# Neighbourhood attention in a two-layer diffusion step: steps of one query block for both heads of a pair, score products in turn on the two halves of the array's rows

## The chip, the cores and the metric

The kernel runs on one core of one Trainium2 chip, as one program launched once. The metric is the device time of that core in microseconds (us): the median over runs, smaller is better. TensorE is PE in the profile (its weight loads PEld), VectorE is DVE, ScalarE is ACT, GpSimd is POOL, SyncE is SP.

## What is computed

Two layers of a hybrid backbone over 640 tokens of width 1024: 512 latent tokens (an 8 by 64 grid) and 128 context tokens. Each layer is a norm and a modulation, one wide input projection, two mixers side by side (retention and neighbourhood attention), gates, an output projection and a SwiGLU feed-forward. The change lies in neighbourhood attention alone. Cut to what matters, for 8 heads of 64 features:

```python
# latent tokens: a window of 8 rows x 16 columns, and 128 cached context keys
s_loc = einsum('bwhd,bwkhd->bhwk', q, k_window) + bias
s_ctx = einsum('bwhd,bshd->bhws', q, k_ctx)
p = softmax(concatenate([s_loc, s_ctx], -1))
o = einsum('bhwk,bwkhd->bwhd', p[..., :n], v_window) + einsum('bhwk,bkhd->bwhd', p[..., n:], v_ctx)
# the 128 context tokens attend to one another
p = softmax(einsum('bqhd,bkhd->bhqk', q, k)); o = einsum('bhqk,bkhd->bqhd', p, v)
```

All inputs are float32. Each large product is made of three reduced-precision ones: both operands are split into a high and a low part (`...h`, `...l`), and high*high, high*low and low*high are added up.

## The kernel before

**Engines and order.** It is written by hand in one function, `build`, with one instruction stream for each engine and semaphores between them. The order on each engine is the order of the code.

**Weights.** They come in 276 slabs of 128 x 1024 (512 KB), 138 a layer, in the order in which PE uses them. SP starts the transfer of slab i into `raw[slot[i]]` (L826) as soon as the slab that last used this slot is done (`prior[i]`, L360 to L368). ACT makes the high part (`wh`, L942), DVE the low part (`wl`, L1280), both by calls of `split(n)` that stand at fixed places of their streams. `wl` and `raw` of a slot are the same memory. Four slots (0 to 3) are always there; four more (4 to 7) lie over memory that neighbourhood attention uses, and are open from slab `WIDE` = 58 of a layer on. Slabs 40 and 41 of a layer are the queries and keys of the first pair of heads, 42 to 45 the values of all heads (two slabs for each call of `values()`), 46 to 53 eight further columns of 128 outputs that are computed inside the attention loop, 54 and 55 two gate columns behind it, 56 and 57 the first half of the attention's output projection.

**Ahead of the loop.** PE runs two columns and then `values()` twice, each some 14 us. ACT and DVE turn the first values into high and low parts, then make a `split(2)` (ACT L942), which is slabs 46 and 47, then split the cached values and keys (L1141, L1143), ACT negates the biases (`negative_bias`, L1115) and loads the table of Exp (L1147), and only then do both take the second values (`nv`, L1129). PE's first score waits for the release of the second values' unit.

**The loop.** For each layer it takes 40 steps g (4 pairs, 2 heads, 5 blocks): four blocks of 128 latent queries and one block of the 128 context queries. A step on PE is `score(g)` (L630: into bank `sc[g % 2]`), some pieces of a column, `turn(g - 1)` (L650: transposes of the probabilities into `tp[g % 2]`), and on some steps `weigh(head, group)` (L661: probabilities by values). A head has 64 features, so its score products use 64 of the array's 128 rows. A block has 3 or 4 tiles of 128 keys, the last of them the cached context; the context block has one. The column pieces (`half_columns`, L613) are 32 a pair: 8 for each half of two columns, each of three products of 128*128 by 320. They are the queries and keys of the next pair, and for the last pair two gate columns. `pieces` (L347) tells how many are due in a step, `LIN_AT` when ACT and DVE take a finished half from one of two banks (`lin_free`).

DVE adds the bias and takes the minimum in one instruction (L1598), ACT does the exponential with its sum (L1167), DVE takes the reciprocal and multiplies (L1602, L1604), PE transposes, ACT makes the high part (`pth`, L1191), DVE the low part (`ptl`, L1290). ACT and DVE add the two halves of each head's output (L1180, L1613). `split` calls in the loop: 2 at g = 0, then 1 at g = 8, 13, 18, 23, 28, 33 and 38.

POOL loads each head's biases whole (640 KB) into one of two buffers.

Of the kernel before, what the change touches and what calls it, by code (L numbers as in the profile page):

```python
# [7 lines left out]
P = 128  # L8
# [7 lines left out]
NPAIR = 4  # L16
# [13 lines left out]
WIDE, W_O, LAST = 58, 64, 130  # L30
# [28 lines left out]
STEPS = NPAIR * 10  # L59
# [47 lines left out]
def build(nc, x_in, w_main, w_first, w_ada, params, decay, state_in, ctx_k, ctx_v, biases, ccol, cvec,  # L107
# [3 lines left out]
    with ctx:  # L111
# [118 lines left out]
        bias = [n0(f"bias{i}", [P, BIASW]) for i in range(2)]  # L230
        s_at = n0.p - Z
# [5 lines left out]

        n1 = Map(ada_at)
        pth = n1("pth", [P, 2, 2, NS], F32R); ptl = n1("ptl", [P, 2, 2, NS], F32R)
# [71 lines left out]
        bias_in = [sem(f"bias_in{i}") for i in range(2)]  # L311
# [29 lines left out]
        STREAMS = ((0, slice(0, NS)), (1, slice(NS, T)))  # L341
        EARLY, CONSTS = 16 * 4, 16 * 3
# [4 lines left out]
        def pieces(p, v):  # L347

            return min(32, -(-(v + 1) * 33 // 10)) if p < NPAIR - 1 else min(32, -(-(v + 1) * 8 // 3))


        LIN_AT = [[3, 5, 7, 10]] * (NPAIR - 1) + [[3, 6, 9, 12]]

        def halves_at(g):

            return [(p, h) for p in range(NPAIR) for h in range(4) if p * 10 + LIN_AT[p][h] == g]

# [27 lines left out]
        def _(pe):  # L385
# [127 lines left out]
            for l in range(DEPTH):  # L513
# [116 lines left out]
                def score(g):  # L630
                    p, v = divmod(g, 10)
                    hh, j = divmod(v, 5)
                    if g >= 2:
                        pe.wait_ge(s_ready, l * STEPS + g - 1)
                    if p >= 1 and v < 2:
                        pe.wait_ge(lin_free[v], l * 8 + 2 * p)
                    nqh, nql, nkh, nkl = nqk[p % 2]
                    rows = slice(64 * hh, 64 * hh + 64)
                    if j < 4:
                        first, tiles, _ = BLOCKS[j]  # L640
                        n = tiles * P
                        q = [t[rows, j * P:(j + 1) * P] for t in (nqh, nql)]
                        product(sc[g % 2][:, 0:n], q, [t[rows, first * P:first * P + n] for t in (nkh, nkl)], True, True)
                        mm = product(sc[g % 2][:, n:n + P], q, [t[rows, p, :] for t in (ckh, ckl)], True, True)
                    else:
                        mm = product(sc[g % 2][:, 0:P], [t[rows, NS:T] for t in (nqh, nql)],
                                     [t[rows, NS:T] for t in (nkh, nkl)], True, True)
                    mm.then_inc(nsc_ready, 1)

                def turn(g):  # L650
                    j = g % 5
                    pe.wait_ge(d_ready, l * STEPS + g + 1)
                    if g >= 2:
                        pe.wait_ge(pt_ready, l * STEPS + g - 1)
                    tiles = [BLOCKS[j][0] + i for i in range(BLOCKS[j][1])] + ["ctx"] if j < 4 else [4]
                    for i, t in enumerate(tiles):
                        to = PLACE[j][t] if j < 4 else 0
                        mm = pe.transpose(tp[g % 2][:, to * P:(to + 1) * P], s[:, g % 2, i * P:(i + 1) * P], ident[:, :])
                    mm.then_inc(t_ready, 1)

                def weigh(head, group):  # L661


                    pe.wait_ge(pt_ready, l * STEPS + head * 5 + (2, 4, 5)[group])
                    if group == 0:
                        pe.wait_ge(av_free, l * 2 * NPAIR + head)

                    def vals(t):
                        return (cv_ if t == "ctx" else nv[:, t])[:, head // 2, head % 2 * 2:head % 2 * 2 + 2, :].rearrange("p b n -> p (b n)")

                    if group == 2:
                        parts = [(vals(4), av[:, 1, 0:P], pch[:, :], pcl[:, :])]
                    else:
                        odd = (1, 0)[group]
                        only = av[:, 0, (group * 2 + odd) * P:(group * 2 + odd + 1) * P]
                        both = av[:, 0, group * 2 * P:(group * 2 + 2) * P]
                        parts = [(vals("ctx"), both, pth[:, group, :, 0:P], ptl[:, group, :, 0:P]),
                                 (vals(2 - group), only, pth[:, group, odd, 3 * P:], ptl[:, group, odd, 3 * P:])]
                        for i in range(2):
                            at_ = slice((i + 1) * P, (i + 2) * P)  # L680
                            parts.append((vals(group * 2 + i), both, pth[:, group, :, at_], ptl[:, group, :, at_]))
                    for i, (val, out, hi, lo) in enumerate(parts):
                        pe.matmul(out, val, hi, start=i == 0, stop=False)
                        mm = pe.matmul(out, val, lo, start=False, stop=i == len(parts) - 1)
# [1152 lines left out]
```

## Time and profile before

| what | before |
|---|---|
| median of 3 runs | 2387.56 us (2384.54 to 4027.47) |
| the profiled execution: its own time | 2394.6 us |
| its span, first to last instruction | 2392.8 us |
| PE busy | 2295.8 us, 96% of the span |
| PE weight loads busy | 2138.3 us, 89% |
| DVE busy | 1303.6 us, 54% |
| ACT busy | 856.7 us, 36% |
| POOL busy | 85.8 us, 4% |
| mean granted TensorE clock | 0.985 |

Neighbourhood attention (first score to first column behind the loop) stands at 476.95 to 614.10 us in the first layer and at 1642.36 to 1777.84 us in the second. To read it: PE is busy nearly always, so the time is what PE is given to do plus the stretches in which it waits. Matmul records overlap, since matmuls are pipelined: the distance between the starts of two neighbours says what one costs, its own duration does not.

### The profile page before, as it was taken

To read this page: it belongs to the slowest core of one execution; us is meant where nothing else is said; L and a number is where in the kernel's file an instruction comes from. 1 tells how busy PE (TensorE), PEld (TensorE's weight loads), DVE (VectorE), ACT (ScalarE), POOL (GpSimd) and SP (SyncE) were. 2 spreads that over 40 slices of the span, in tenths; PEclk is the share of its full clock that TensorE was granted. 3 is DMA by queue.
4 is the path that set the end of the run, shared out by engine and by line. 5 is a ranking of instruction groups with operands and counts; after the bars stand their busy time and mean duration, and the time that the engine had idled before them with its cause. 6 is when DMAs were issued, how large, how long until landed. Compare 5 with 4: busy or idle time off the path is not lost.

```text
span 2392.8 us, 33465 instructions
## 1 busy us (share of the span) xinstructions
PE 2295.8 (96%) x14296; PEld 2138.3 (89%) x14296; DVE 1303.6 (54%) x1867; ACT 856.7 (36%) x1359; POOL 85.8 (4%) x161
## 2 busy tenths in 40 slices
PE   7999988999989999999979999999999999999997
PEld 3999988988978999999969999999989799999996
DVE  3555567566756767667464555424655534343344
ACT  4544432245335212221265444324553432221212
POOL 0000001000000000000000000000000000000000
PEclk9999999999999999999999999999999999999999
DMA  5211145322443443433412111222222322222121
GB/s 240 84 62 58 58 143 180 104 82 66 164 106 123 156 144 125 158 123 124 106 45 80 58 62 58 71 91 80 82 89 90 116 80 80 73 69 83 59 88 44
DMA packets 59747, 233.57 MB, mean 98 GB/s; under 512 B 7312, under 2 KB 7344, under 8 KB 57424
## 3 DMA queue, kind: packets, MB, share of 16 engines
q1 hardware_dynamic: 41040, 153.12, 19.7%
q0 software_dynamic: 18560, 78.33, 9.5%
q8 instruction: 113, 1.85, 0.3%
q14 instruction: 34, 0.28, 0.0%
HBM read 223.00 MB, written 8.42 MB: 97 GB/s over the span
## 4 chain that ended last, share of the span: by engine, by line
PE 80%; DVE 10%; ACT 4%; issue 2%; DMA 2%; DVEq 1%; ACTq 0%; SPq 0%; POOL 0%; POOLq 0%
PE unit L402 15%; PE unit L403 15%; PE unit L405 15%; PE unit L390 9%; PE unit L392 9%; PE unit L391 9%; DVE junk L1380 2%; DMA raw<-w_main 1%; PE unit L483 1%; DVE rs L1414 1%; PE sc L390 1%; PE unit L519 1%; DVE wl L1280 1%; DVE ptl L1290 1%; PE sc L392 1%
## 5 line engine op out<-in xcount | busy, mean ns | idle before, releaser
L402 PE MATMUL unit<-hmh,wh 128*128 128x320 f32 x2304 | 696.5, 310 | 11.6 <-DVE vl L1290 10.4
L403 PE MATMUL unit<-hml,wh 128*128 128x320 f32 x2304 | 694.0, 309 | 0.0
L1280 DVE TENSOR_TENSOR wl<-raw,wh 128x1024 fp32r<-128x1024 f32 x276 | 335.2, 1222 | 411.3 <-ACT wh L942 405.1
L405 PE MATMUL unit<-hmh,wl 128*128 128x320 f32 x2304 | 525.0, 309 | 0.0
L402 PEld LDWEIGHTS unit<-hmh,wh 128*128 128x128 f32 x2304 | 432.6, 188 | 16.4 <-issue 14.4
L403 PEld LDWEIGHTS unit<-hml,wh 128*128 128x128 f32 x2304 | 432.7, 188 | 2.0
L405 PEld LDWEIGHTS unit<-hmh,wl 128*128 128x128 f32 x2304 | 385.4, 188 | 0.0
L942 ACT ACTIVATE wh<-raw 128x1024 fp32r<-128x1024 f32 x276 | 283.8, 1049 | 118.8 <-DMA raw<-w_main 118.6
L1380 DVE CUSTOM_DVE_ANT_0 junk<-ada,csb,par 128x1024 f32<-128x1024 f32 x160 | 205.5, 1284 | 24.9 <-DMA ada<-w_ada 4.4
L390 PE MATMUL unit<-wh,hmh 128*128 128x256 f32 (+1 forms) x640 | 203.0, 317 | 10.9 <-DVE hml L1290 4.7
L392 PE MATMUL unit<-wh,hml 128*128 128x256 f32 (+1 forms) x640 | 200.8, 314 | 0.0
L391 PE MATMUL unit<-wl,hmh 128*128 128x256 f32 (+1 forms) x640 | 200.7, 314 | 0.0
L390 PE MATMUL unit<-wh,hidh 128*128 128x512 f32 x440 | 172.9, 393 | 0.0
L392 PE MATMUL unit<-wh,hidl 128*128 128x512 f32 x440 | 172.6, 392 | 0.0
L391 PE MATMUL unit<-wl,hidh 128*128 128x512 f32 x440 | 172.5, 392 | 0.0
L1237 ACT ACTIVATE sig<-unit 128x640 f32<-128x640 f32 (+2 forms) x46 | 31.1, 681 | 384.2 <-PE unit L405 380.2
L390 PE MATMUL unit<-hmh,wh 128*128 128x320 f32 (+2 forms) x384 | 131.6, 343 | 14.4 <-DVE hml L1290 14.4
L390 PEld LDWEIGHTS unit<-wh,hmh 128*128 128x128 f32 x640 | 123.6, 193 | 20.1 <-DVE wl L1280 5.1
L1242 ACT ACTIVATE hidh<-sig 128x640 fp32r<-128x640 f32 x44 | 32.5, 739 | 287.5 <-DVE sig L1680 287.5
L392 PEld LDWEIGHTS unit<-wh,hml 128*128 128x128 f32 x640 | 123.5, 193 | 7.3
L391 PEld LDWEIGHTS unit<-wl,hmh 128*128 128x128 f32 x640 | 123.3, 193 | 7.2
L1697 DVE TENSOR_TENSOR mix<-unit,mix 128x1024 f32<-128x1024 f32 x80 | 97.8, 1223 | 46.0 <-PE unit L392 46.0
(283 smaller groups left out, 3461.2 us busy)
## 6 DMA issues: line engine op xcount, KB each, us to landing
raw<-w_main SPq DMA_DIRECT2D x276, 512.0 KB, 3.6
ada<-w_ada POOLq DMA_DIRECT2D x80, 512.0 KB, 3.9
bias<-biases POOLq DMA_DIRECT2D x16, 640.0 KB, 5.1
first<-w_first SPq DMA_DIRECT2D x8, 1024.0 KB, 21.1
x<-x POOLq DMA_DIRECT2D x2, 2560.0 KB, 11.9
gains<-g_rows POOLq DMA_DIRECT2D x4, 1024.0 KB, 5.0
x_keep<-x POOLq DMA_DIRECT2D x1, 2560.0 KB, 8.9
x<-x_keep POOLq DMA_DIRECT2D x1, 2560.0 KB, 9.5
```

Of the source, the lines that this page charges most:

```text
L390: pe.matmul(out, a[0], b[0], start=first, stop=False)
L391: pe.matmul(out, a[0], b[1], start=False, stop=False)
L392: return pe.matmul(out, a[1], b[0], start=False, stop=last)
L402: pe.matmul(u[:, h, 0:n], a[0], xs[h][0], start=f, stop=False)
L403: pe.matmul(u[:, h, 0:n], a[0], xs[h][1], start=False, stop=False)
L405: mm = pe.matmul(u[:, h, 0:n], a[1], xs[h][0], start=False, stop=z)
L942: act.activation(wh[slot[i]][:, :], raw[slot[i]][:, :], ACT.Copy).then_inc(w_hi[slot[i]], 1)
L1237: a = act.activation(part, of, ACT.Silu)
L1242: act.activation(hidh[:, b % 2, n, :], sig[:, :], ACT.Copy).then_inc(hid_hi, 1)
L1280: dve.tensor_tensor(wl[slot[i]][:, :], raw[slot[i]][:, :], f32(wh[slot[i]][:, :]), ALU.subtract)\
L1380: a = dve.tensor_tensor_reduce(junk[:, :], ada[i % ADA_RING][:, :], csb[:, which, :], 1.0, par[:, l, B_ADA + chunk:B_ADA + chunk + 1], ALU ...
L1697: U.release(dve.tensor_tensor(mix[:, t, :], flat(u[:, :, :]), mix[:, t, :], ALU.add))
```

## The change

One step i (20 a layer: 4 pairs, 5 blocks) now takes the same block of both heads of a pair.

- `score(i)`: the products of head 0 (rows 0 to 63 of the array, bank `sc[0]`) and of head 1 (rows 64 to 127, bank `sc[1]`) are issued in turn. Count and shapes of the products are the same.
- `turn(i - 1)` stands directly behind `score(i)`, ahead of the column pieces. `weigh` does both heads, one behind the other, in steps 5p+3, 5p+5 and 5p+6.
- Each head has its own transposed probabilities: `pth[1]` and `ptl[1]` lie over the memory of weight slots 2 and 3. So slabs 46 to 55 (`NARROW` to `WIDE`) use slots 0 and 1 only, and `WIDE` is 56.
- `split` calls in the loop: 1 at i = 4, 6, 9, 11, 14, 16 and 20, and two more behind it.
- Biases are loaded and negated in three kinds apart. The outputs of a head are added in two parts, of 256 and 384 columns.

```diff
-WIDE, W_O, LAST = 58, 64, 130
+NARROW, WIDE, W_O, LAST = 46, 56, 64, 130
-STEPS = NPAIR * 10
+STEPS = NPAIR * 5
-        pth = n1("pth", [P, 2, 2, NS], F32R); ptl = n1("ptl", [P, 2, 2, NS], F32R)
+        pth = [n1("pth", [P, 2, 2, NS], F32R), at("pth1", [P, 2, 2, NS], wl_at + (RING + 2) * SLAB * 4, F32R)]
+        ptl = [n1("ptl", [P, 2, 2, NS], F32R), at("ptl1", [P, 2, 2, NS], wl_at + 2 * SLAB * 4, F32R)]
...
+        def pieces(p, j):
+            return min(32, -(-(j + 1) * 33 // 5)) if p < NPAIR - 1 else min(32, -(-(j + 1) * 32 // 7))
+        LIN_AT = [[1, 2, 3, 4]] * (NPAIR - 1) + [[1, 3, 5, 6]]
+        def weighed_at(i):
+            return [(p, group) for p in range(NPAIR) for group in range(3) if p * 5 + (3, 5, 6)[group] == i]
+        def sums_at(i):
+            return [(p, half) for p in range(NPAIR) for half in range(2) if p * 5 + (4, 7)[half] == i]
+        SPLIT_AT = (4, 6, 9, 11, 14, 16, 20)
...
-            may = range(RING) if j < WIDE or LAST <= j < LAST + 4 else range(RING, RING + MORE) if j >= LAST - 2 else range(RING + MORE)
+            may = range(2) if NARROW <= j < WIDE else range(RING) if j < WIDE or LAST <= j < LAST + 4 else range(RING, RING + MORE) if j >= LAST - 2 else range(RING + MORE)
...
+                def score(i):
+                    p, j = divmod(i, 5)
+                    pe.wait_ge(s_ready, (l * STEPS + i) * 2)
+                    if p >= 1 and j < 2:
+                        pe.wait_ge(lin_free[j], l * 8 + 2 * p)
+                    rows = [slice(64 * hh, 64 * hh + 64) for hh in range(2)]
+                    terms = ((0, 0), (0, 1), (1, 0))
+                    if j < 4:
+                        for t, (a, b) in enumerate(terms):
+                            for hh in range(2):
+                                pe.matmul(sc[hh][:, 0:n], (nqh, nql)[a][rows[hh], j * P:(j + 1) * P],
+                                          (nkh, nkl)[b][rows[hh], first * P:first * P + n], start=t == 0, stop=t == 2)
...
                 pe.wait_ge(cv_ready, l + 1)
+                for i in range(STEPS + 2):
...
+                    if i < STEPS:
+                        score(i)
+                    if 1 <= i <= STEPS:
+                        turn(i - 1)
+                    due = pieces(p, j)
+                    for _ in range(due - done):
+                        next(source)
...
+                    for q, group in weighed_at(i):
+                        for hh in range(2):
+                            weigh(q, group, hh)
...
+                for i in range(STEPS + 3):
+                    if 1 <= i <= STEPS:
+                        turned_high(i - 1, 0)
+                    if i < STEPS:
+                        for hh in range(2):
+                            act.wait_ge(s_ready, (l * STEPS + i) * 2 + hh + 1)
+                            act.activation(s[:, hh, 0:n], s[:, hh, 0:n], ACT.Exp, bias=nmax[:, v:v + 1], scale=-1.0,
+                                           accum_out=sums[:, v:v + 1]).then_inc(e_ready, 1)
+                    if 1 <= i <= STEPS:
+                        turned_high(i - 1, 1)
+                    for q, h in halves_at(i):
+                        half_column(q, h)
+                    for q, half in sums_at(i):
+                        act.activation(avs[there, cols], av[here, hh, of], ACT.Copy).then_inc(av_half, 1)
+                    if i in SPLIT_AT:
                         split()
```

The last hunk is ACT's stream; DVE's has the matching calls at the same places, with `normalise` (reciprocal and multiplication) where ACT has the exponential.

The first place is SP's queue from slab 42 of the first layer on (`raw0` to `raw3` are the slots).

```order
L826 DMA raw2_57<-w_main 128x1024 [waits unit_ready]
L826 DMA raw3_58<-w_main 128x1024 [waits unit_ready]
L826 DMA raw0_55<-w_main 128x1024 [waits unit_ready]
L826 DMA raw1_56<-w_main 128x1024 [waits unit_ready]
L826 DMA raw2_57<-w_main 128x1024 [waits unit_ready]
L826 DMA raw3_58<-w_main 128x1024 [waits unit_ready]
```

In the change the same six transfers, slabs 42 to 47, are these:

```order
L854 DMA raw2_57<-w_main 128x1024 [waits unit_ready]
L854 DMA raw3_58<-w_main 128x1024 [waits unit_ready]
L854 DMA raw0_55<-w_main 128x1024 [waits unit_ready]
L854 DMA raw1_56<-w_main 128x1024 [waits unit_ready]
L854 DMA raw0_55<-w_main 128x1024 [waits unit_ready]
L854 DMA raw1_56<-w_main 128x1024 [waits unit_ready]
```

The last two, slabs 46 and 47, went into slots 2 and 3 (last used by slabs 42 and 43, the first values); they now go into slots 0 and 1 (last used by slabs 44 and 45, the second values).

The second place is PE at the start of the loop. Before, one head's scores and then the pieces:

```order
L390 MATMUL sc<-nkh_132,nqh_130 128x256 [waits cv_ready,ck_ready,unit_free0]
L391 MATMUL sc<-nkl_133,nqh_130 128x256
L392 MATMUL sc<-nkh_132,nql_131 128x256
L390 MATMUL sc<-ckh,nqh_130 128x128
L391 MATMUL sc<-ckl,nqh_130 128x128
L392 MATMUL sc<-ckh,nql_131 128x128
L390 MATMUL unit<-hmh,wh_61 128x320 [waits lin_free0,w_lo2]
```

In the change, steps 0 and 1 of both heads (of the 21 piece products between them the first stands here):

```order
L667 MATMUL sc<-nkh_132,nqh_130 128x256 [waits cv_ready,s_ready,ck_ready,unit_free0]
L667 MATMUL sc<-nkh_132,nqh_130 128x256
L667 MATMUL sc<-nkl_133,nqh_130 128x256 x2
L667 MATMUL sc<-nkh_132,nql_131 128x256 x2
L671 MATMUL sc<-ckh,nqh_130 128x128 x2
L671 MATMUL sc<-ckl,nqh_130 128x128 x2
L671 MATMUL sc<-ckh,nql_131 128x128 x2
L413 MATMUL unit<-hmh,wh_59 128x320 [waits lin_free0,w_lo0]
```

Two products of like names follow one another, one of each head, and the first piece waits for the low part in slot 0 instead of slot 2.

The third place is ACT between the first and the second values; it reads the same before and after but for the slots (`w_in2`, `w_in3` before) and the biases' width. In the change:

```order
L971 ACTIVATE wh_59<-raw_55 128x1024 [waits w_in0]
L971 ACTIVATE wh_60<-raw_56 128x1024 [waits w_in1]
L1172 ACTIVATE cv__141<-cvr 128x4x2x64 [waits cv_in]
L1174 ACTIVATE ckh<-ckr 128x512 [waits ck_in]
L1146 ACTIVATE bias_145<-bias_145 128x384 [waits bias_in00]
L1146 ACTIVATE bias_146<-bias_146 128x384 [waits bias_in10]
L1177 ACT_TABLE_LOAD
L1177 ACTIVATE flag_a<-epsc 128x1
L1160 ACTIVATE nv<-unit 128x2x2x64 [waits unit_ready]
```

ACT's two splits of slabs 46 and 47 stand ahead of its first instruction on the second values (`nv`, the last row), as they did before.

## Rows read from the trace of the kernel before

**Rows 1.** The page: span and busiest engine
```profile
span 2392.8 us, 33465 instructions
...
PE 2295.8 (96%) x14296; PEld 2138.3 (89%) x14296; DVE 1303.6 (54%) x1867; ACT 856.7 (36%) x1359; POOL 85.8 (4%) x161
```

**Rows 2.** Busy time by stretch (busy us and count of each engine, clock, DMA share, GB/s)
```profile
477.00:490.00 13.00, 11.29 (x64) 10.01 (x64) 7.53 (x18) 5.97 (x12) 0.55 (x1) 0.88 0.33 101
490.00:510.00 20.00, 20.00 (x129) 18.89 (x128) 10.68 (x32) 8.03 (x20) 0.53 (x1) 0.91 0.17 60
510.00:530.00 20.00, 19.11 (x131) 17.63 (x131) 13.45 (x35) 12.38 (x27) 1.08 (x3) 1.00 0.21 65
```

**Rows 3.** Waits of PE over the whole span: total us, times, longest
```profile
PE sc L390 <- DVE nkl L1584: 5.9, 6, 1.2
...
PE tp L658 <- DVE s L1604: 3.7, 4, 1.7
```

**Rows 4.** Timeline of PE, first layer's attention: start, us, line, op
```profile
476.75 0.28 PE L392 MATMUL unit<-wh,hml 128*128 128x256 f32 x1
476.95 0.38 PE L390 MATMUL sc<-nkh,nqh 64*128 64x256 f32 x1
477.18 0.28 PE L391 MATMUL sc<-nkl,nqh 64*128 64x256 f32 x1
...
477.42 0.22 PE L390 MATMUL sc<-ckh,nqh 64*128 64x128 f32 x1
477.48 0.27 PE L391 MATMUL sc<-ckl,nqh 64*128 64x128 f32 x1
477.59 0.27 PE L392 MATMUL sc<-ckh,nql 64*128 64x128 f32 x1
477.79 0.41 PE L390 MATMUL unit<-hmh,wh 128*128 128x320 f32 x1
478.04 0.31 PE L391 MATMUL unit<-hml,wh 128*128 128x320 f32 x1
478.19 0.31 PE L392 MATMUL unit<-hmh,wl 128*128 128x320 f32 x1
...
479.75 0.45 PE L390 MATMUL sc<-nkh,nqh 64*128 64x384 f32 x1
...
480.75 0.41 PE L390 MATMUL unit<-hmh,wh 128*128 128x320 f32 x1
...
494.71 0.32 PE L390 MATMUL sc<-nkh,nqh 64*128 64x128 f32 x1
...
495.19 0.42 PE L390 MATMUL unit<-hmh,wh 128*128 128x320 f32 x1
...
614.10 0.38 PE L402 MATMUL unit<-hmh,wh 128*128 128x320 f32 x1 [0.40 <-issue]
```

**Rows 5.** Timeline of ACT around the second values, [idle before <- what ended it]
```profile
467.40 1.06 ACT L942 ACTIVATE wh<-raw 128x1024 fp32r<-128x1024 f32 x1 [0.20 <-DMA raw<-w_main]
...
469.41 2.42 ACT L1115 ACTIVATE bias<-bias 128x1280 f32<-128x1280 f32 x2
471.84 1.28 ACT L1147 ACT_TABLE_LOAD   x1
...
474.19 1.21 ACT L1129 ACTIVATE nv<-unit 128x256 fp32r<-128x256 f32 x4 [0.85 <-PE unit L392]
...
481.04 1.06 ACT L942 ACTIVATE wh<-raw 128x1024 fp32r<-128x1024 f32 x1 [1.35 <-DMA raw<-w_main]
482.34 1.06 ACT L942 ACTIVATE wh<-raw 128x1024 fp32r<-128x1024 f32 x1 [0.24 <-DMA raw<-w_main]
```

**Rows 6.** Timeline of DVE, the second values
```profile
475.43 1.41 DVE L1290 TENSOR_TENSOR nv<-unit,nv 128x256 fp32r<-128x256 f32 x4 [4.51 <-ACT nv L1129]
```

**Rows 7.** Timelines of ACT and of DVE around the end of the first pair
```profile
515.88 0.26 ACT L1111 ACTIVATE nkst<-unit 128x128 f32<-128x128 f32 x1
516.04 0.43 ACT L1158 ACTIVATE nkh<-unit 128x320 fp32r<-128x320 f32 x1
...
522.86 0.69 ACT L1180 ACTIVATE avs<-unit 64x640 f32<-64x640 f32 x1
...
527.65 1.23 DVE L1280 TENSOR_TENSOR wl<-raw,wh 128x1024 fp32r<-128x1024 f32 x1 [0.25 <-ACT wh L942]
```

More of the change, by code:

```diff
@@ L341, in build @@
         STREAMS = ((0, slice(0, NS)), (1, slice(NS, T)))
+        BIAS_AT = [slice(KIND_AT[n], KIND_AT[n] + KIND_W[n] + P) for n in range(3)]
         EARLY, CONSTS = 16 * 4, 16 * 3
@@ new lines, in score @@
+                        for t, (a, b) in enumerate(terms):
+                            for hh in range(2):
+                                mm = pe.matmul(sc[hh][:, n:n + P], (nqh, nql)[a][rows[hh], j * P:(j + 1) * P],
+                                               (ckh, ckl)[b][rows[hh], p, :], start=t == 0, stop=t == 2)
+                    else:
+                        for t, (a, b) in enumerate(terms):
+                            for hh in range(2):
+                                mm = pe.matmul(sc[hh][:, 0:P], (nqh, nql)[a][rows[hh], NS:T], (nkh, nkl)[b][rows[hh], NS:T],
+                                               start=t == 0, stop=t == 2)
@@ L648, in score @@
                     mm.then_inc(nsc_ready, 1)
[L650 to L659, printed above, removed]
@@ L661, in weigh, with turn @@
-                def weigh(head, group):
-                    pe.wait_ge(pt_ready, l * STEPS + head * 5 + (2, 4, 5)[group])
+                def turn(i):
+                    j = i % 5
+                    tiles = [BLOCKS[j][0] + n for n in range(BLOCKS[j][1])] + ["ctx"] if j < 4 else [4]
+                    for hh in range(2):
+                        g = (l * STEPS + i) * 2 + hh
+                        pe.wait_ge(d_ready, g + 1)
+                        if g >= 2:
+                            pe.wait_ge(pt_ready, g - 1)
+                        for n, t in enumerate(tiles):
+                            to = PLACE[j][t] if j < 4 else 0
+                            mm = pe.transpose(tp[hh][:, to * P:(to + 1) * P], s[:, hh, n * P:(n + 1) * P], ident[:, :])
+                        mm.then_inc(t_ready, 1)
@@ L671, in weigh @@
                     if group == 2:
-                        parts = [(vals(4), av[:, 1, 0:P], pch[:, :], pcl[:, :])]
+                        parts = [(vals(4), to, pch[hh][:, :], pcl[hh][:, :])]
                     else:
                         odd = (1, 0)[group]
[L675 to L684, printed above, removed]
+                        parts = [(vals("ctx"), to, pth[hh][:, group, :, 0:P], ptl[hh][:, group, :, 0:P]),
+                                 (vals(2 - group), to[:, odd * P:(odd + 1) * P], pth[hh][:, group, odd, 3 * P:], ptl[hh][:, group, odd, 3 * P:])]
@@ L685, in weigh @@
+                        for n in range(2):
+                            at_ = slice((n + 1) * P, (n + 2) * P)
+                            parts.append((vals(group * 2 + n), to, pth[hh][:, group, :, at_], ptl[hh][:, group, :, at_]))
+                    for n, (val, out, hi, lo) in enumerate(parts):
+                        pe.matmul(out, val, hi, start=n == 0, stop=False)
+                        mm = pe.matmul(out, val, lo, start=False, stop=n == len(parts) - 1)
                     mm.then_inc(pt_done, 1)
@@ L1111, in keys_of_context, with negative_biases @@
                     act.activation(nkst[:, p % 2, :], view, ACT.Copy).then_inc(nkst_ready, 1)
-                def negative_bias(head):
-                    act.wait_ge(bias_in[head % 2], (l * NPAIR + head // 2 + 1) * 16)
-                    act.activation(bias[head % 2][:, :], bias[head % 2][:, :], ACT.Copy, scale=-1.0).then_inc(bias_ready, 1)
+                def negative_biases(p, kind):
+                    for hh in range(2):
+                        at_ = BIAS_AT[kind]
+                        act.wait_ge(bias_in[hh][kind], (l * NPAIR + p + 1) * 16)
+                        act.activation(bias[hh][:, at_], bias[hh][:, at_], ACT.Copy, scale=-1.0).then_inc(bias_ready, 1)
                 for to, scale in ((nqk[0][0], -Q_SCALE), (nqk[0][2], 1.0)):
@@ L1143, in _ @@
                         act.activation(ckh[:, :, :], ckr[:, :, :], ACT.Copy).then_inc(ck_hi, 1)
-                        for head in range(2):
-                            negative_bias(head)
+                        negative_biases(0, 0)
                         act.activation(flag_a[:, :], epsc[:, :], ACT.Exp)
@@ L1625, in _ @@
                     lo(ynl[:, c, :], yna[:, c, :], ynh[:, c, :]).then_inc(yn_ready, 1)
+                split()
                 if l == 0:
```

221 lines of the change are left out of this document (103 added, 118 removed).

## The prediction

> **What bounds the kernel now.** I read the page first, then the busy time by stretch, the waits of PE, and the timelines around neighbourhood attention. The page shows PE busy for 2295.8 of 2392.8 us [rows 1]. The stretches show the same inside attention: from 510 to 530 us PE is busy for 19.11 of 20 us, DVE for 13.45 and ACT for 12.38 [rows 2]. So there too time goes only where PE is given less, or waits less. Attention runs from 476.95 to 614.10 us in the first layer [rows 4], 137.15 us; the second layer's is alike. Twice that is 274 us, 11% of the span, and nothing outside it is changed except which slot a few weight slabs take. A change of over 2% (48 us), about what a measurement of this kernel can tell from no change, would need 24 us in each layer, a sixth of the stage.
>
> What PE waits for in the loop is small. The table of PE's waits has 5.9 us in six waits of a score for the low part of the next pair's keys, and 3.7 us in four waits of a transpose for the probabilities [rows 3]; both are sums over two layers.
>
> **Scores.** The timeline of PE prices one head's score [rows 4]. With 256 keys and the context it takes 477.79 - 476.95 = 0.84 us, with 384 keys 480.75 - 479.75 = 1.00, the context block 495.19 - 494.71 = 0.48. A pair has 4, 4 and 2 of these: 8.32 us. Of each call some 0.2 us is passing between 128-row and 64-row products: the first score product starts 0.20 after its forerunner and the next one 0.23 after it, where neighbours of 256 columns stand 0.12 apart. The first column piece behind a call stands 0.25 ahead of its neighbour, against 0.15 for the next one: another 0.1. A pair's calls fall from 10 to 5, so 5 x 0.2 = 1.0 us and 5 x 0.1 = 0.5 us go.
>
> What is left, 8.32 - 10 x 0.2 = 6.32 us a pair, is products with their weight loads, and here the trace shows no two row halves in turn, so I bound it. Upper end: nothing overlaps, 6.32 stays. Lower end: two halves run side by side entirely, 3.16. Between them stands a row: products of 128 columns start 477.59 - 477.48 = 0.11 us apart, though half the columns of 256 should need half of 0.12; so a load with its product seems to cost 0.11, whatever the columns. Each of a step's 12 (6 in the context block) has its own load. If the products overlap and the loads do not, a pair is (4 x 12 + 6) x 0.11 = 5.94 us. I take this, as the only one with a row: scores fall by 1.0 + 0.38 = 1.38 us a pair, 5.5 a layer, and with the 0.1 of each piece 2.0 more. Full overlap gives 4 x (5.94 - 3.16) = 11.1 us a layer beyond that, no overlap takes 1.5 back.
>
> The Trainium skill, TensorE: Matmul & The Clock Gate, LDWEIGHTS, says that a load takes its columns over 1.2 GHz whatever the rows, 107 ns for 128: by that, and one load at a time, a pair is 54 x 0.107 = 5.8 us, and the rows' 0.11 agrees. The same page, Part 3 (Packing small matmuls), says that matmuls on different row groups run concurrently and that a load overlaps with a matmul in flight if the row groups differ; no row here shows it, and it is the second rival below.
>
> **Transposes, weighing, pieces.** Their products are the same in number and shape. `turn` now stands before the pieces, but its input has by then had the whole former step, about 6 us of PE, and the exchange DVE, ACT, DVE of two heads lies beside pieces and weighing. So the 3.7 us of transpose waits go (1.85 a layer), and the 5.9 us of waits for the keys too (2.95 a layer), since the score that needs the last half column is a full step later. I give 0.5 a layer back for the last pair, whose steps have only 4 or 5 pieces. DVE (67%) and ACT (62%) get some calls more and no more elements, and stay under PE [rows 2].
>
> **The weight slots, first place: the start of the loop.** This is what speaks against the change. Slabs 46 and 47 now need slots 0 and 1, free only when the second `values()` has ended on PE, at about 476.95 [rows 4]. Slabs 48 and 49 had this very condition before, and ACT could start on them at 481.04 and 482.34 us [rows 5]: those are the moments at which slabs 46 and 47 now arrive. But in ACT's order their two splits stand ahead of the second values' high parts, and PE's first score waits for the release of that unit. So the whole of PE waits. I replay ACT's row from 482.34: split, values and keys of the context 469.41 - 467.40 = 2.01 us, so 484.35; biases, 2 x 384 of the former 2 x 1280 columns, 2.42 x 0.3 = 0.7, I take 0.8, so 485.15; table load 1.28, so 486.4; second values 1.21, so 487.6 [rows 5]; DVE's low parts 1.41 behind, and 0.1 to the score, so 489.2 [rows 6]. PE starts at 489.2 instead of 476.95: 12.3 us a layer. Nothing covers it, as the pieces need slab 46 too. Bounds: ACT's splits were 0.2 us from the landing, so with transfers a us earlier or later 11 to 14.
>
> **Second place: the pair boundaries.** In steps 5, 10 and 15 the first piece needs slab 48, 50 or 52, split at i = 4, 9 or 14 and there behind the last half column, which PE ends in the same step. From that end, t: ACT hears of it after 0.2, copies the context keys and the half (516.04 - 515.88 = 0.16, then some 0.35), adds two output parts of 256 columns (0.69 for 640, so about 0.6 for both), splits (1.06), and DVE makes the low part (1.23) [rows 5, 7]: t + 3.6. PE meanwhile has the score (0.2 + 12 x 0.11 = 1.5) and two short transposes (0.4): t + 1.9. It waits 1.7 us, three times a layer: 5.1 us. With faster scores it waits longer, up to 2.4 each.
>
> The last slot effect, slab 55 behind the loop, has PE's column of slab 54 as cover (48 products of 0.147, 7 us); transfer and split need about the same, so I count 0 and keep 1 us for the upper end.
>
> **The clock.** In the first layer the granted clock is 0.88 from 477 to 490 us and 0.91 in the next 20 [rows 2], after the loop's first waits: part of the time at 1.2 instead of 2.4 GHz, 0.12 x 13 + 0.09 x 20 = 3.4 us lost. A stop of 12 us will bring the low level again, but takes the place of this one. I count 0, from -2 to +3 a layer.
>
> **Sum, a layer:** +12.3 (start) + 5.1 (boundaries) + 0.5 - 5.5 (scores) - 2.0 (pieces behind scores) - 1.85 - 2.95 = +5.6 us; both layers +11.2. The profiled execution's own time is 2394.6, 1.8 above its span and 7.0 above the median: it would be 2405.8, and the median 2387.56 + 11.2 = 2398.8.
>
> **Rivals.** (a) *The halves overlap entirely*, loads too. Then scores give 11.1 us a layer more, of which the boundaries take back 3 x 0.7 = 2: +5.6 - 9.1 = -3.5 a layer, 2387.56 - 7.0 = 2380.6, faster than before by 0.3%. For it: the two halves share neither rows nor banks. Against: no load in these rows is nearer than 0.1 us to its neighbour but the 0.06 between 477.42 and 477.48, where the load had been made ahead [rows 4]. By the page on packing this is what should happen.
>
> (b) *Passing from one half to the other costs what passing from 128 to 64 rows costs*, 0.2 us, as each product in turn changes rows. 54 passages a pair are 10.8 us, and nothing overlaps: against my sum + 10.8 + 0.4 a pair, 45 a layer, +90 in all: 2489, slower by 4%. It decides from about 0.1 us a passage on. For it: the 0.20 and 0.23 of the rows. Against: those change the size of the tile too. The Trainium skill, TensorEngine Tiling (Array Packing), Key Properties, says "Changing tiling mode (not just tile) drains the TensorE": by that (b) is out.
>
> (c) *The start does not stall*, because I misread what the slabs wait for. Then 5.6 - 12.3 = -6.7 a layer, 2374. Against: the queue's order has slots 0 and 1 there.
>
> **How the numbers follow.** My forecast, loads one at a time with both stalls: 0.5. (a) or something on the way to it: 0.35. (b), or a mix of small penalties: 0.07. (c): 0.08. The range goes from 2376, where (a) with a bettered clock lies, to 2420, my sum with the upper ends (12.3 to 14, no overlap 1.5, clock 3, slab 55 1: +7.2 a layer, 2413) and some spread between runs. Over 2% faster needs (a) and (c) together and no waits at the boundaries either: 2387.56 - 2 x (6.7 + 11.1 + 5.1) = 2341.8, still just short of it; 0.02. Over 2% slower is (b): 0.05. Within 2%: 0.93.
>
> **What would show it.** Right: PE idle for 11 to 14 us ahead of the first score of each layer, released by DVE's `nv`, with ACT waiting for the transfer of `raw`; three waits of some 1.7 us of a piece for `wl` in steps 5, 10, 15; score products of the two heads with starts 0.1 us apart on average, a step's score at 1.5 us; no more waits of a score for `nkl`; the stage at about 143 us. Wrong: starts in couples a few ns apart and a step's score under 1.1 us is (a); gaps of 0.2 us between the halves are (b); a first score at once behind the second values is (c). Transposes that wait for DVE in the middle pairs would show that I took the exchange between the engines too lightly.

## The result, and the profile after

The change makes the kernel faster by 0.85%: 2368.61 us median of 6 runs (2366.72 to 2371.03) against 2386.32 for the kernel before in its 6 runs, one of which took 4027.47 us and has no part in the ratio. The ratio on record is 0.9915, 95% interval 0.9901 to 0.9928; the two medians alone give 0.9926, a gain of 17.7 us, and the ratio some 20. I had forecast 2398.8, a loss of 0.5%, within 2376 to 2420. The time lies under the range, and the sign was wrong.

The page of the changed kernel, against [rows 1]:

```profile
span 2364.9 us, 33540 instructions
...
PE 2255.6 (95%) x14296; PEld 2107.7 (89%) x14296; DVE 1298.5 (55%) x1883; ACT 858.1 (36%) x1407; POOL 103.0 (4%) x193
```

PE is busy 40.2 us less with the same 14296 products, so records now lie on top of one another that lay side by side. The profiled execution's own time is 2366.72, 27.9 under that of before; the medians differ by 17.7. The profiled execution of before took 8.3 us more than its median and that of the change 1.9 less, so the spans overstate the gain by 10 us.

PE's waits after, against [rows 3] (total us, times, longest):

```profile
PE unit L413 <- DVE wl L1322: 15.8, 6, 2.6
...
PE sc L667 <- DVE nv L1332: 11.7, 1, 11.7
...
PE tp L690 <- DVE ptl L1332: 2.0, 4, 0.6
...
PE tp L690 <- DVE s L1642: 0.5, 2, 0.3
```

Both waits that the forecast feared are there, but the one of 11.7 us stands once and not twice. The 5.9 us of a score for the keys are gone, and of the 3.7 us of a transpose for the probabilities (`s`) 0.5 are left. The 2.0 us of a transpose for `ptl` are new.

The timeline of PE, two of the first layer's steps with what stands around them, against [rows 4]:

```profile
474.41 0.28 PE L415 MATMUL unit<-wh,hml 128*128 128x256 f32 x1
486.42 0.58 PE L667 MATMUL sc<-nkh,nqh 64*128 64x256 f32 x2 [11.73 <-DVE nv L1332]
...
497.67 0.44 PE L667 MATMUL sc<-nkh,nqh 64*128 64x384 f32 x2
497.95 0.34 PE L667 MATMUL sc<-nkl,nqh 64*128 64x384 f32 x2
498.13 0.34 PE L667 MATMUL sc<-nkh,nql 64*128 64x384 f32 x2
498.30 0.22 PE L671 MATMUL sc<-ckh,nqh 64*128 64x128 f32 x2
498.36 0.28 PE L671 MATMUL sc<-ckl,nqh 64*128 64x128 f32 x2
498.48 0.28 PE L671 MATMUL sc<-ckh,nql 64*128 64x128 f32 x2
498.68 1.09 PE L690 MATMUL tp<-ident,s 128*128 128x128 f32 x8
499.53 0.39 PE L413 MATMUL unit<-hmh,wh 128*128 128x320 f32 x1
499.76 0.31 PE L414 MATMUL unit<-hml,wh 128*128 128x320 f32 x1
```

Each row of a score is two products, one of each head, and the two together last what one lasted: 0.44 us for a first product of 384 columns, against 0.45 for a single one before. The step's twelve products take 498.68 - 497.67 = 1.01 us, one head's call of before (1.00). The weight loads of the same step, PEld in the timeline, come in twos as well, each at one time:

```profile
497.67 0.19 PEld L667 LDWEIGHTS sc<-nkh,nqh 64*128 64x128 f32 x2 [0.19 <-issue]
497.78 0.19 PEld L667 LDWEIGHTS sc<-nkl,nqh 64*128 64x128 f32 x2
```

So products and weight loads of the two halves run side by side entirely: rival (a).

The wait of 11.73 us comes by the way that the forecast replayed. ACT's timeline has the split of slab 46, which waited for its transfer, and the second values behind it:

```profile
478.15 1.06 ACT L971 ACTIVATE wh<-raw 128x1024 fp32r<-128x1024 f32 x1 [17.36 <-DMA raw<-w_main]
...
483.73 1.19 ACT L1160 ACTIVATE nv<-unit 128x256 fp32r<-128x256 f32 x4
```

The second layer's start has no wait:

```profile
1632.98 0.28 PE L415 MATMUL unit<-wh,hml 128*128 128x256 f32 x1
1633.19 0.39 PE L667 MATMUL sc<-nkh,nqh 64*128 64x256 f32 x2
```

The end of the first pair, against [rows 7]. ACT's timeline:

```profile
512.73 0.28 ACT L1140 ACTIVATE nkst<-unit 128x128 f32<-128x128 f32 x1 [0.80 <-PE unit L415]
512.90 0.43 ACT L1188 ACTIVATE nkh<-unit 128x320 fp32r<-128x320 f32 x1
513.36 0.78 ACT L1226 ACTIVATE avs<-unit 64x256 f32<-64x256 f32 x2
514.16 1.06 ACT L971 ACTIVATE wh<-raw 128x1024 fp32r<-128x1024 f32 x1
```

DVE's:

```profile
515.25 1.23 DVE L1322 TENSOR_TENSOR wl<-raw,wh 128x1024 fp32r<-128x1024 f32 x1 [0.60 <-ACT wh L971]
```

And PE's:

```profile
513.46 0.44 PE L690 MATMUL tp<-ident,s 128*128 128x128 f32 x2
516.53 0.63 PE L413 MATMUL unit<-hmh,wh 128*128 128x320 f32 x1 [2.63 <-DVE wl L1322]
```

It is the chain that the forecast walked: half column, output parts, split, low part, then the piece.

**Where the time went.** I added up the distances between the starts of neighbours on PE over the second layer's stage, from first score to first column behind. Both sums hold the waits.

| us, second layer | before | after |
|---|---|---|
| scores | 33.0 | 17.0 |
| transposes | 14.4 | 22.5, of it 7.9 waits for `wl` |
| weighing | 24.2, of it 2.9 waits for `nkl` | 18.2 |
| column pieces | 63.9, of it 1.7 waits for `s` | 63.1 |
| the stage | 135.5 | 120.8 |

(The timeline puts a wait on what ran before it: that for `wl` on the transposes, that for `nkl` on the weighing.) So 14.7 us are won in the second layer. In the first the stage falls from 137.15 to 124.04, and 11.8 are lost ahead of it: 1.3 won. Together 16.0 of the median's 17.7. In the profiled executions the stretch between the two attention stages got shorter too, 1022.73 us against 1028.26, though the change leaves PE's work there alone. Its largest part is one wait behind the attention that varies from execution to execution (experiment 6), so I don't count it as the change's.

### The profile page after: what moved, and what is told of

It is laid out like the page before. It is cut to its first block, busy times and chain, and to the rows that moved or that the text cites. A ratio compares the mean times of both kernels' runs of the same rounds, so it can differ in the third digit from the quotient of the medians.

```text
span 2364.9 us, 33540 instructions
## 1 busy us (share of the span) xinstructions
PE 2255.6 (95%) x14296; PEld 2107.7 (89%) x14296; DVE 1298.5 (55%) x1883; ACT 858.1 (36%) x1407; POOL 103.0 (4%) x193
## 4 chain that ended last, share of the span: by engine, by line
PE 83%; DVE 8%; ACT 4%; DMA 2%; issue 2%; DVEq 1%; ACTq 0%; SPq 0%; POOL 0%; POOLq 0%
PE unit L425 16%; PE unit L426 16%; PE unit L428 16%; PE unit L413 10%; PE unit L414 10%; PE unit L415 10%; DVE junk L1422 2%; PE tp L690 1%; DVE rs L1456 1%; DVE wl L1322 1%; DMA first<-w_first 1%; PE unit L542 1%; DMA raw<-w_main 1%; PE unit L717 1%; PE unit L716 1%
## 5 line engine op out<-in xcount | busy, mean ns | idle before, releaser
L425 PE MATMUL unit<-hmh,wh 128*128 128x320 f32 x2304 | 696.6, 310 | 11.1 <-DVE vl L1332 10.4
L413 PE MATMUL unit<-hmh,wh 128*128 128x320 f32 (+2 forms) x384 | 129.4, 337 | 30.1 <-DVE wl L1322 15.8
L414 PE MATMUL unit<-hml,wh 128*128 128x320 f32 (+2 forms) x384 | 125.0, 325 | 0.0
## 6 DMA issues: line engine op xcount, KB each, us to landing
x<-x POOLq DMA_DIRECT2D x2, 2560.0 KB, 11.9
```

The costliest lines, as they stand in the source:

```text
L413: pe.matmul(out, a[0], b[0], start=first, stop=False)
L414: pe.matmul(out, a[0], b[1], start=False, stop=False)
L425: pe.matmul(u[:, h, 0:n], a[0], xs[h][0], start=f, stop=False)
```

## The experiments

Each kernel is the change with one edit. Ratios are to the kernel before, run on the same chip; the change itself has 0.9915, and a difference of 0.001 in ratio is 2.4 us. The differences below are taken from the ratios. Those of the plain medians are up to 5 us apart from them, so a difference of a few us says little.

**1. Heads apart, by threes.** The loops over term and head change places:

```diff
-                        for t, (a, b) in enumerate(terms):
-                            for hh in range(2):
+                        for hh in range(2):
+                            for t, (a, b) in enumerate(terms):
```

> The change, with the three score products of head 0 issued one behind the other and then the three of head 1 (the window's keys, then the same for the context's), instead of in turn. Count, shapes, banks and waits are the same. Theory A (the two halves of the rows run side by side only when neighbours in the stream are on different halves): scores go back from 17.7 us a layer to 4 x (6.3 + 1.0) = 29, the time rises by some 20 to 24 us against the change's 2368.6, and starts stand 0.12 and 0.17 us apart again. Theory B (the saving is from fewer passages between 128 and 64 rows, or the array pairs the halves by itself): within 5 us of the change.

Measured 2369.16 us, ratio 0.9911 (0.9894 to 0.9928): no difference. The timeline of this kernel, a step of 384 columns:

```profile
498.37 0.45 PE L667 MATMUL sc<-nkh,nqh 64*128 64x384 f32 x2
498.65 0.34 PE L667 MATMUL sc<-nkl,nqh 64*128 64x384 f32 x2
...
499.38 1.09 PE L690 MATMUL tp<-ident,s 128*128 128x128 f32 x8
```

Each row holds two products again, one of each head: head 1's first product starts with head 0's first, although two others stand between them in the stream, and the step takes 1.01 us again. Theory B held in its second form: the array pairs the halves by itself. Issuing in turn, which the change is named for, is worth nothing against three and three; how far apart the two halves may stand is the next experiment.

**2. All six apart.** Head 0's window and context products, then head 1's.

```diff
-                        for t, (a, b) in enumerate(terms):
-                            for hh in range(2):
+                        for hh in range(2):
+                            for t, (a, b) in enumerate(terms):
...
-                        for t, (a, b) in enumerate(terms):
-                            for hh in range(2):
+                            for t, (a, b) in enumerate(terms):
```

> The change, with all six score products of head 0 (window and context) issued one behind the other, and then all six of head 1. In the run with three and three apart the time did not move. Theory A (each half of the rows works off its own products as they come, over at least six of the stream's products): a step's score stays at 1.0 us and the time within 4 us of the change. Theory B (the pairing reaches only over a few products): part of the overlap goes, up to 1.6 us a step more, 8 to 60 us in all.

Measured 2384.14 us, ratio 0.9961 (0.9940 to 0.9983), some 11 us over the change. Its timeline:

```profile
498.29 0.44 PE L667 MATMUL sc<-nkh,nqh 64*128 64x384 f32 x1
498.57 0.34 PE L667 MATMUL sc<-nkl,nqh 64*128 64x384 f32 x1
498.75 0.33 PE L667 MATMUL sc<-nkh,nql 64*128 64x384 f32 x1
498.75 0.44 PE L667 MATMUL sc<-nkh,nqh 64*128 64x384 f32 x1
498.92 0.22 PE L670 MATMUL sc<-ckh,nqh 64*128 64x128 f32 x1
...
499.76 1.09 PE L689 MATMUL tp<-ident,s 128*128 128x128 f32 x8
```

Head 1's first product, seventh in the stream, starts at 498.75 together with head 0's third. So here it passed three others still to come, and not five: the reach has an end, theory B. It is so in all 32 steps with a window, and the time from head 0's first product to its third does not matter: it is 0.34 us with 256 keys, 0.46 with 384 and 0.59 in the first step of the first layer, at the low clock. That speaks for a count of products and against a time; what sets the count stays open. A step of 384 keys takes 1.47 us instead of 1.01, the first layer's scores 24.1 us instead of 17.7.

The Trainium skill, TensorE: Matmul & The Clock Gate, Part 3 (Packing small matmuls), says that matmuls on different row groups run concurrently, and the 0.44 us for two agree. It also has them start and end strictly in the stream's order; the starts in the rows of these two runs show otherwise where the row halves differ.

**3. Transposes between the heads.** The overlap taken away, and with it the saving of passages between 128-row and 64-row products:

```diff
+                    for hh in range(2):
+                        if i < STEPS:
+                            score(i, hh)
+                        if 1 <= i <= STEPS:
+                            turn(i - 1, hh)
```

> The change, with the scores of a step taken apart by head: head 0's scores, head 0's transposes, head 1's scores, head 1's transposes. The transposes use all 128 rows, so that the two halves' products are no longer neighbours; work and waits stay (the product that tells VectorE is the last of head 1). Theory A (the gain of the change is that products on the two halves run side by side, for whichever order they are issued in within a block): scores go back to some 33 us a layer, the time rises by 28 to 36 us. Theory B (it comes from fewer waits and from weighing two heads in a row): under 12 us, for the passages between row modes.

Measured 2404.29 us, ratio 1.0055 (1.0040 to 1.0070): 33 us over the change, as theory A had it. The timeline shows single products again:

```profile
504.67 0.39 PE L667 MATMUL sc<-nkh,nqh 64*128 64x256 f32 x1
504.90 0.28 PE L667 MATMUL sc<-nkl,nqh 64*128 64x256 f32 x1
...
505.51 0.66 PE L688 MATMUL tp<-ident,s 128*128 128x128 f32 x4
506.10 0.38 PE L667 MATMUL sc<-nkh,nqh 64*128 64x256 f32 x1
```

The first layer's scores cost 33.6 us against 17.7, and both layers' 31.6 us more than in the change. Not all of this is the overlap: a pair has ten score calls between 128-row products again and not five, and at the forecast's 0.2 us a call that is 4 us a layer, so the overlap itself is some 24 of the 31.6 (an estimate). The waits for `wl` fell meanwhile, from 15.8 to 10.0 us, as the longer scores cover more. The kernel is slower than before by 0.55%, 13 us. The no-overlap end of my sum, +5.6 + 1.5 a layer less one start stall of 12, is +2; the extra passages are 8 of the 11 us between, and what the rest is was not told apart.

**4. The split one step earlier.**

```diff
-        SPLIT_AT = (4, 6, 9, 11, 14, 16, 20)
+        SPLIT_AT = (3, 6, 8, 11, 13, 16, 20)
```

> The change, with the splits of slabs 48, 50 and 52 one step earlier (i = 3, 8, 13 instead of 4, 9, 14), ahead of the last half column. Theory A (the six waits of 2.63 us at the pair boundaries come from the split standing behind the half column that TensorE ends in the same step): they go, 15.8 us, and with them the low clock behind some of them: 16 to 21 us less. Theory B (the slab's slot is free and its transfer landed too late for that step, so ScalarE waits there and delays the rest): under 8 us less, or a loss.

Measured 2347.76 us, ratio 0.9822 (0.9807 to 0.9837): 22 us under the change, theory A, a little over its upper end. No wait for `wl` is left in the loop. The stretches of the change and then of this kernel show what went with them (the figure behind the five engines is the granted clock; the last two rows of each are the whole stages):

```profile
514.00:530.00 16.00, 13.47 (x86) 13.19 (x88) 8.37 (x25) 7.69 (x19) 1.06 (x2) 0.79 0.20 61
...
1650.00:1670.00 20.00, 17.37 (x129) 16.45 (x128) 9.97 (x32) 8.56 (x24) 2.69 (x5) 0.91 0.24 70
...
486.42:610.46 124.04, 114.72 (x864) 108.98 (x865) 80.11 (x234) 72.20 (x183) 11.41 (x22) 0.92 0.21 67
...
1633.19:1753.97 120.78, 111.47 (x866) 105.79 (x865) 80.26 (x234) 72.88 (x185) 12.38 (x23) 0.96 0.22 69
```

```profile
514.00:530.00 16.00, 16.00 (x133) 15.41 (x132) 11.57 (x34) 11.19 (x29) 2.67 (x5) 1.00 0.31 91
...
487.78:597.45 109.67, 108.24 (x864) 103.22 (x865) 80.02 (x234) 71.94 (x183) 11.41 (x22) 0.98 0.24 75
...
1626.69:1734.16 107.47, 106.05 (x865) 101.07 (x865) 80.18 (x234) 72.60 (x185) 12.37 (x23) 1.00 0.25 77
```

Each wait of 2.63 us is followed by a stretch in which part of the time runs at 1.2 GHz: 0.21 x 16 = 3.4 us lost around the first, 0.09 x 20 = 1.8 around the second layer's first, and 0.11 x 16 = 1.8 around each of the other four; without the waits nothing is lost there. The two stages are 14.37 and 13.31 us shorter, 27.7 together. Of these 15.8 are the waits, so 11.9 are the clock. Outside the stages this execution is 7.8 us longer than the change's, most of it (6.5 us) between the two stages, where the edit changes nothing; the cause of that is open, and it hides part of the gain.

**5. The start: values' slabs placed by hand.**

```diff
-            may = range(2) if NARROW <= j < WIDE else range(RING) if j < WIDE or LAST <= j < LAST + 4 else range(RING, RING + MORE) if j >= LAST - 2 else range(RING + MORE)
+            may = range(2) if j in (42, 43) or NARROW <= j < WIDE else range(2, 4) if j in (44, 45) else range(RING) if j < WIDE or LAST <= j < LAST + 4 else range(RING, RING + MORE) if j >= LAST - 2 else range(RING + MORE)
```

> The change, with the second values' slabs (44, 45) in slots 2 and 3 and the first values' (42, 43) in slots 0 and 1 in both layers, so that slabs 46 and 47 wait for the first values only. The second layer's rotation already falls so; only the first layer's changes. Theory A (the 11.7 us idle of TensorE ahead of the first layer's scores is this slot wait and nothing else): the first score follows the values at once, the time falls by 11 to 14 us. Theory B (another wait stands right behind it, as for the biases or the load of slab 48): falls by under 6 us.

Measured 2370.93 us, ratio 0.9922 (0.9901 to 0.9942): nothing won, theory B. The waits of PE say why:

```profile
PE unit L413 <- DVE wl L1322: 22.7, 7, 7.0
```

The 11.7 us are gone, but a seventh wait of 7.0 us is new, ahead of the first values: slabs 42 and 43 now follow 40 and 41 directly into their slots, as 46 and 47 had followed 44 and 45. The wait was moved. From PE's wait for `merged` (418.15 us here, 415.26 in the change) to the first score it is 68.7 us against 71.2, so 2.5 us are won by that count and none in the median.

**6. The start: the whole rotation turned by two.**

```diff
-            may = range(2) if NARROW <= j < WIDE else range(RING) if j < WIDE or LAST <= j < LAST + 4 else range(RING, RING + MORE) if j >= LAST - 2 else range(RING + MORE)
+            may = range(2, 4) if i < 2 else range(2) if i < 4 or NARROW <= j < WIDE else range(RING) if j < WIDE or LAST <= j < LAST + 4 else range(RING, RING + MORE) if j >= LAST - 2 else range(RING + MORE)
```

> The change, with the rotation of the first layer's slots turned by two from the first slab on (slabs 0 and 1 in slots 2 and 3, 2 and 3 in 0 and 1), so that each slab up to 45 still follows the fourth before it, and 46 and 47 follow 42 and 43 as in the second layer. Theory A (the 11.7 us ahead of the first layer's scores are the slot wait, and the run with slabs 42 to 45 placed by hand only moved it to the values, 7.0 us there): no wait over 3 us at either place in the first layer, and 11 to 15 us less than the change. Theory B (the stall had cover, as the equal time of that run could also mean): under 5 us.

Measured 2363.54 us, ratio 0.9889 (0.9874 to 0.9904): some 6 us under the change, less than theory A's 11 to 15. The wait is gone, and none has taken its place ahead of the loop: from PE's wait for `merged` at 416.23 us to the end of the stage it is 597.63 - 416.23 = 181.4 us, against 610.46 - 415.26 = 195.2 in the change. But most of those 13.8 us do not reach the end in this execution. A column behind the output projection waits longer for DVE, here and then in the change:

```profile
682.67 0.77 PE L413 MATMUL unit<-wh,hmh 128*128 128x512 f32 x1 [4.80 <-DVE hml L1332]
```

```profile
690.59 0.47 PE L413 MATMUL unit<-wh,hmh 128*128 128x512 f32 x1 [0.45 <-DVE hml L1332]
```

The granted clock from 680 to 700 us and from 700 to 780 is 0.83 and 0.96 here and 1.00 in both stretches of the change, another 0.17 x 20 + 0.04 x 80 = 6.6 us. Wait and clock together are 11 us, and between the two attention stages this execution is 10.0 us longer than the change's. The wait was 4.69 us before the change too, and 4.05 in experiment 1, whose edit leaves the slots as they are, with the clock at 0.91 and 0.96 in the same stretches. So it varies between kernels that do the same there, the change's profiled execution had it at its shortest (0.45 us), and the 6 us measured here are no measure of the slot wait. Experiment 9 has a better one.

**7. The second layer's start stalled too.**

```diff
-            may = range(2) if NARROW <= j < WIDE else range(RING) if j < WIDE or LAST <= j < LAST + 4 else range(RING, RING + MORE) if j >= LAST - 2 else range(RING + MORE)
+            may = range(2) if NARROW <= j < WIDE or j in (44, 45) else range(2, 4) if j in (42, 43) else range(RING) if j < WIDE or LAST <= j < LAST + 4 else range(RING, RING + MORE) if j >= LAST - 2 else range(RING + MORE)
```

> The change, with slabs 44 and 45 in slots 0 and 1 and 42 and 43 in slots 2 and 3 in both layers, so that the second layer too has slabs 46 and 47 behind its second values, as the forecast took it to be. Theory A (the forecast counted this stall twice where the rotation of slots gives it once): TensorE idles some 12 us ahead of the second layer's scores too, the time rises by 11 to 14 us against the change. Theory B (the second layer has cover that the first lacks): under 4 us.

Measured 2395.71 us, ratio 1.0023 (1.0012 to 1.0035): 26 us over the change, more than either theory. The waits of PE in this kernel:

```profile
PE sc L667 <- DVE nv L1332: 24.0, 2, 12.1
PE unit L413 <- DVE wl L1322: 23.1, 7, 7.4
```

The stall stands twice, as the forecast assumed, and there is the wait of experiment 5 besides, which I had not foreseen: 12.3 + 7.3 = 19.6 us of new waits. Behind them the clock was lower (0.92 over the second layer's stage, against 0.96 in the change), which fits the rest but was not tried by itself. The stall has no cover in the second layer; the rotation of the slots alone spares it.

**8. Transposes late.**

```diff
-                    if 1 <= i <= STEPS:
-                        turn(i - 1)
                     due = pieces(p, j)
                     for _ in range(due - done):
                         next(source)
                     done = due
+                    if 1 <= i <= STEPS:
+                        turn(i - 1)
```

> The change, with the transposes of the former step behind the column pieces, where they stood before, instead of ahead of them. Theory A (each head has a single buffer for its probabilities, so VectorE's next minimum waits for the transposes, and a score waits for that minimum): new waits of a score for VectorE in the steps without weighing, 1 to 2 us each in some 10 steps a layer, 15 to 35 us more. Theory B (the place does not matter, there is slack): within 4 us of the change.

Measured 2417.80 us, ratio 1.0103 (1.0081 to 1.0125), 45 us over the change. The waits:

```profile
PE unit L413 <- DVE wl L1322: 29.6, 10, 3.8
...
PE sc L667 <- DVE nmax L1655: 18.7, 22, 1.2
```

Theory A: with one buffer of probabilities for each head, DVE's minimum waits for the transposes, and 22 scores wait for DVE. The size went past the expectation, as the pair boundaries grew as well, from 15.8 us in 6 waits to 29.6 in 10. The place of `turn` is a part of the change that its gain needs; I had booked it as a small plus.

**9. Both mends.** Experiments 4 and 6 together.

> The turned rotation together with the early splits (i = 3, 8, 13). If the two waits are independent, the gains add: 12 and 21 us, so some 33 under the change, near 2335 by the first runs' scale, ratio to before 0.977 to 0.980. If one covers part of the other, ratio 0.982 as with the early splits alone.

Measured 2335.27 us, ratio 0.9768 (0.9754 to 0.9783): 2.3% faster than before, 35 us under the change. The turned rotation is worth 13 us on top of the early split, about what its wait had cost. That is more than the 6 us that it gave by itself in experiment 6, so the two don't add up from the single runs (22 + 6 = 28). The two stages of this kernel:

```profile
474.47:581.93 107.46, 106.04 (x866) 101.06 (x865) 80.19 (x234) 72.61 (x185) 12.35 (x23) 1.00 0.25 77
...
1611.44:1718.90 107.46, 106.04 (x865) 101.06 (x865) 80.19 (x234) 72.59 (x185) 12.37 (x23) 1.00 0.25 77
```

PE waits for 1.4 us of each and the clock never falls, where before it was 0.88 and 0.91 in the first 33 us [rows 2]. The stage takes 107.5 us in either layer, against 137.15 and 135.48 before the change.

## Why the prediction was wrong

**What bounds the kernel: right.** PE bounds it, and the stage is the place. DVE and ACT stayed under PE.

**Scores: the step that failed first.** "If the products overlap and the loads do not, a pair is (4 x 12 + 6) x 0.11 = 5.94 us. I take this, as the only one with a row". Loads overlap as well. The row (0.11 us between products of 128 columns) told of one row half only; nothing in it spoke of a load on the other. I forecast 5.5 us a layer from the scores. Measured are 16.0, and the lower end of my own bounds, 5.5 + 11.1 = 16.6, hits it. The Trainium skill, TensorE: Matmul & The Clock Gate, Part 3 (Packing small matmuls), which I set aside to a rival, says that matmuls on different row groups run concurrently, and the trace agrees. I should have seen that "the only one with a row" was a row about another case.

**The start: the step that failed second.** "PE starts at 489.2 instead of 476.95: 12.3 us a layer." In the first layer it was 11.7 us idle, by the chain as I walked it. But "a layer" was false. Walking the slot rule of the code gives slots 2, 3, 0, 1 for slabs 42 to 45 in both layers before the change. In the changed kernel the second layer has them in 0, 1, 2, 3, as the narrowed stretch leaves the rotation turned by two. So there 46 and 47 still follow 42 and 43. I had read SP's queue of the first layer only, and rival (c), which would have caught half of this, took both layers at once. Experiments 5 to 7 show that the stall is this wait.

With these two put right, my own terms give 5.6 - 11.1 + 2.1 = -3.4 for the first layer and -15.7 for the second, together -19: 2368 from the 2387.56 that I started from. Measured: 2368.61. Those two steps explain the side of the miss and nearly all of its size, but that the sum then comes so near is luck. By layer the stage and the stall ahead of it gave -1.3 and -14.7, and smaller terms were off both ways:

- *Boundaries*: 1.7 us each, or up to 2.4 with faster scores; they were 2.63. The chain from PE's last piece was 4.0 us and not 3.6: the two output parts took 0.80 and not 0.6, the copy of the half column 0.46 and not 0.35.
- *The clock*: counted at 0. The boundary waits cost 11.9 us of clock beyond their own 15.8 (experiment 4). The stages had a granted clock of 0.98 and 0.99 before and 0.92 and 0.96 in the change, so against before the clock cost some 6 to 7 us more in the first layer and 3 to 4 in the second, over my bound of 3.
- *Weighing*: not priced at all. A head's eight products took 1.1 us alone and the two heads' sixteen take 1.94 in a row. Without its waits weighing fell from some 21 to 18.2 us a layer, which about offsets the clock in the second.
- *Waits for keys and transposes*: 5.9 us gone, as forecast; of the 3.7 us 0.5 stayed. New are 2.0 us for `ptl`, in the last pair, where I had left 1.0.
- *Pieces behind scores*: 2.0 a layer forecast. The first piece behind other work still stands 0.23 ahead of its neighbour, now behind transposes, but in 21 places a layer instead of 40 at 0.25. Against 0.15 for a common piece that is 4.0 - 1.7 = 2.3 us: about as forecast.
- *Slab 55*: no wait for `wl` stands behind the loop, 0 as forecast.

**The rivals.** (a) happened, and its time of 2380.6 had the start stall once too often. (b), the passage between halves at 0.2 us, is refuted by every row of two products: they start at one time. The range failed because (a) and half of (c) came together, which it did not hold.

## What to carry to other kernels

Products that use different halves of the array's rows need only stand near one another in the stream and not in turn: three and three cost nothing here, six and six cost 11 us. 128-row work between them takes the overlap away; that and the extra passages cost 33 us. When a change takes buffers from a ring, walk every user of the ring in each pass of the loop, up to the first that wraps: the phase of the rotation can differ between passes, and a mend that moves one user only may move the wait. Six waits of 2.63 us on TensorE cost 15.8 us and 11.9 more for the clock behind them: price such a wait at its own length and three quarters again, as an estimate.

## What the runs showed of the hardware

Two products with their own weight loads, on rows 0 to 63 and 64 to 127, take together what one takes: 0.44 us against 0.45 for the first of 384 columns, 1.01 against 1.00 us for a whole block. A product on the other half started ahead of products issued before it: past two in experiment 1, past three, and never more, in experiment 2. My forecast had one weight load at a time. Waits of 2.63 us were followed by a lower granted clock (0.79 in 514 to 530 us), and without them it was 1.00.
